# A two-layer hybrid decoder: where the recurrence's gate products stand, and which operand of the attention values is turned

## The chip, the core and the metric

The program runs on one core of a Trainium2 chip. The time is the device time of one execution in microseconds (us); lower is better. The kernel before took 3752.8 us, the median of three runs (3745.65 to 3756.24). One more execution was taken by the hardware profiler: 3757.68 us, of which the span from the first to the last instruction is 3756.1 us.

## The reference

Two groups of tokens, 256 of a prompt and 8 samples of 8 tokens (320 columns together), go through two layers of width 1024. Two places matter here. The first is the RWKV branch: 3328 columns of the input projection are mixed with the token before, and the last 256 of them feed three small products.

```python
mixed = (rwkv_cols + (prev - rwkv_cols) * p['rwkv_mu'][l]).astype(f32)
r, kc, vc, wd, ad, gd = jnp.split(mixed, RWKV_SPLITS, axis=-1)   # 1024, 1024, 1024, 64, 64, 128
w_log = -jax.nn.softplus(-(p['rwkv_w0'][l] + jnp.tanh(wd) @ p['rwkv_w_w2'][l])) - 0.5
decay = jnp.exp(-jnp.exp(w_log))
a_lr = jax.nn.sigmoid(p['rwkv_a0'][l] + ad @ p['rwkv_w_a2'][l])
g_rw = jax.nn.sigmoid(gd) @ p['rwkv_w_g2'][l]
```

The second is the cross attention, 4 heads of 256 dimensions over 256 memory tokens. The prompt has one memory, each of the 8 samples has its own:

```python
s = jnp.einsum('bthd,bmhd->bhtm', q, mk.astype(h.dtype)).astype(jnp.float32) * (X_HEAD_DIM ** -0.5)
pr = jax.nn.softmax(s, axis=-1).astype(h.dtype)
o = jnp.einsum('bhtm,bmhd->bthd', pr, mv.astype(h.dtype)).reshape(bsz, t, D_MODEL)
```

## The kernel before

Everything lies on chip with 128 features on the partitions and the 320 tokens along the row. A hardware loop runs over the two layers. The weights of a layer come as chunks of 128 output columns (512 KB) through a ring of four slots in the order of the table `SEGS`; SyncE issues the loads. For each chunk ScalarE makes `w_high` (L1330), then VectorE or GpSimd the remainder `w_low` (L1671, L662), and TensorE does 8 x 3 matmuls into one PSUM bank (L808 to L810, or L800, L801 and L805 for a chunk that takes its input in parts). Two split chunks are held (`AHEAD`), so a split starts when the matmuls of the chunk two before it are done (`chunk_done`).

In the segment `rwkv` (26 chunks) GpSimd makes `w_low`, and VectorE mixes the tokens straight from PSUM (`mix_tokens`, L1769 to L1774, five instructions; L1773 alone has both inputs in SBUF). Loops of four chunks drive all engines. The weights of the small products are two more chunks, `lora`, loaded into slots 2 and 3 of the ring. When all 26 chunks are mixed, ScalarE applies tanh and sigmoid to the last two (L1405, L1406), and TensorE computes the products for each of eight column tiles i (L911 to L913), with ScalarE's sigmoids (L1410, L1411) and VectorE's copy of the gate (L1779) behind each. Then VectorE, in `prepare_rwkv`, scales and scans the decay (L1798, L1800), computes `k * k_k` and its square (L1803, L1804), and so on to the recurrence. TensorE does 15 chunks of other projections beside it (`fill_rwkv`, L848 to L850): four, then the head sums of the square (L920), then six, further sums, then five. All fills use one PSUM bank, which ScalarE copies out (L1398). `prepare_rwkv` overwrites the place of the shift state, so it first waits until GpSimd's store of it (L693) has landed. GpSimd issues that store behind its `w_low` of the first two fills.

In the attention the work goes in units: 8 of the prompt (two token tiles by four heads) and 8 of the samples. Each has steps `s` (scores, L1236 or L1243), `max` and `p` on VectorE (L2151, L2152; L2155, L2156), `exp` and `t` on ScalarE (L1576, L1582), `t` on TensorE (transposes, L1251), and `o` (L1259 or L1266). The order on each engine is given by `att_steps`; on TensorE it is s(u+1), t(u), o(u). For a sample the four heads' scores lie in four strips of 32 partitions, 32 rows holding the queries of four samples, of which one's are wanted. The values of a sample are the stationary operand of `o`, in 8 tiles of 128 x 128, with 8 probability columns moving (L1266, N = 8). GpSimd loads keys and values of samples 0 to 3 ahead and issues those of sample 4 + j when `o` of sample j is done (L756, L757), 2 MB for each sample.

## Time and profile before

| | |
|---|---|
| median of three runs | 3752.8 us |
| profiled execution | 3757.68 us |
| its span | 3756.1 us |
| TensorE matmul busy | 3210.9 us (85%) |
| TensorE weight load busy | 2923.7 us (78%) |
| VectorE busy | 1952.9 us (52%) |
| ScalarE busy | 1165.8 us (31%) |
| GpSimd busy | 526.0 us (14%) |
| read from and written to HBM | 397.01 and 48.02 MB |

The profile reports busy time per engine, waits with the instruction that ended them, and the clock granted to TensorE (1.0 is 2.4 GHz, 0.5 is 1.2 GHz). A matmul of these 32-bit operands stands in the trace as two instructions where neither operand is split; order lists of the program count it once. Stages are told apart by line numbers.

### The profile page before, as it was taken

The page shows a single profiled execution, that of the slowest core. Times are in us where ns is not written, and L with a number is a line of the kernel's source. Part 1 is how long each engine was busy: PE and PEld are TensorE (multiplying, and loading weights), DVE is VectorE, ACT ScalarE, POOL GpSimd, SP SyncE. Part 2 cuts the span into 40 slices and gives each one's busy share as a digit, 9 for nine tenths or more (in the row PEclk, how much of TensorE's full clock was granted, in tenths as well). Part 3 has the DMA queues.
Part 4 walks back from the last instruction along what each step waited for, and adds up shares of the span by engine and source line. Part 5 has one row for each costly group of instructions (what it writes and reads, how often), then busy time and mean ns, then how long its engine had stood idle before and what let it go on. Part 6 is the DMA issues. An engine that isn't in the chain of part 4 may idle for free. (4 is left out here: it accounts for less than half of the span.)

```text
span 3756.1 us, 64350 instructions
## 1 busy us (share of the span) xinstructions
PE 3210.9 (85%) x25896; PEld 2923.7 (78%) x25896; DVE 1952.9 (52%) x2902; ACT 1165.8 (31%) x1579; POOL 526.0 (14%) x337
## 2 busy tenths in 40 slices
PE   8999788878877897899989888887788878978997
PEld 7989578577575897799989886775675768867997
DVE  4437565585565554144344476556753755541443
ACT  4432421141131443144344324111421214421442
POOL 0006310242210000000000164102422000000000
PEclk9999899887898999599989999999888979995999
DMA  4444210242262454234344443002422533532343
GB/s 159 150 135 139 92 38 3 68 141 85 61 254 109 143 189 148 90 124 150 118 140 149 134 135 100 24 24 70 150 74 81 212 151 124 187 128 112 130 149 104
DMA packets 119682, 448.03 MB, mean 119 GB/s; under 512 B 13648, under 2 KB 23920, under 8 KB 112176
## 3 DMA queue, kind: packets, MB, share of 16 engines
q1 hardware_dynamic: 98496, 331.84, 27.1%
q0 software_dynamic: 20976, 113.24, 7.7%
q8 instruction: 150, 2.46, 0.3%
q14 instruction: 60, 0.49, 0.1%
HBM read 397.01 MB, written 48.02 MB: 118 GB/s over the span
## 5 line engine op out<-in xcount | busy, mean ns | idle before, releaser
L808 PE MATMUL gemm_banks<-in_high,w_high 128*128 128x320 f32 (+1 forms) x2784 | 874.7, 314 | 76.8 <-POOL w_low L662 28.5
L1330 ACT ACTIVATE w_high<-ring 128x1024 fp32r<-128x1024 f32 x598 | 631.8, 1057 | 967.9 <-PE gemm_banks L810 633.2
L809 PE MATMUL gemm_banks<-in_low,w_high 128*128 128x320 f32 (+1 forms) x2784 | 863.0, 310 | 0.0
L810 PE MATMUL gemm_banks<-in_high,w_low 128*128 128x320 f32 (+1 forms) x2784 | 862.5, 310 | 0.0
L1671 DVE TENSOR_TENSOR w_low<-ring,w_high 128x1024 fp32r<-128x1024 f32 x436 | 533.9, 1225 | 543.8 <-ACT w_high L1330 539.9
L808 PEld LDWEIGHTS gemm_banks<-in_high,w_high 128*128 128x128 f32 x2784 | 531.9, 191 | 94.1 <-issue 74.1
L662 POOL TENSOR_TENSOR w_low<-ring,w_high 128x1024 fp32r<-128x1024 f32 x162 | 419.8, 2593 | 1139.3 <-ACT w_high L1330 623.9
L809 PEld LDWEIGHTS gemm_banks<-in_low,w_high 128*128 128x128 f32 x2784 | 532.3, 191 | 1.1
L810 PEld LDWEIGHTS gemm_banks<-in_high,w_low 128*128 128x128 f32 x2784 | 531.6, 191 | 0.0
L848 PE MATMUL gemm_banks<-in_high,w_high 128*128 128x320 f32 x640 | 227.5, 355 | 66.1 <-ACT stage L1398 41.5
L800 PE MATMUL gemm_banks<-in_high,w_high 128*128 128x320 f32 (+1 forms) x656 | 213.8, 338 | 68.6 <-ACT in_high L1346 65.3
L870 PE MATMUL gemm_banks<-act_high,w_high 128*128 128x320 f32 x704 | 224.7, 319 | 2.5 <-DVE arena L1723 2.5
L872 PE MATMUL gemm_banks<-act_high,w_low 128*128 128x320 f32 x704 | 217.6, 309 | 0.0
L871 PE MATMUL gemm_banks<-act_low,w_high 128*128 128x320 f32 x704 | 217.4, 309 | 0.0
L849 PE MATMUL gemm_banks<-in_low,w_high 128*128 128x320 f32 x640 | 212.7, 332 | 0.0
L850 PE MATMUL gemm_banks<-in_high,w_low 128*128 128x320 f32 x640 | 211.8, 331 | 0.0
L801 PE MATMUL gemm_banks<-in_high,w_low 128*128 128x320 f32 (+1 forms) x656 | 208.6, 330 | 0.0
L848 PEld LDWEIGHTS gemm_banks<-in_high,w_high 128*128 128x128 f32 x640 | 134.9, 211 | 90.6 <-issue 58.2
L800 PEld LDWEIGHTS gemm_banks<-in_high,w_high 128*128 128x128 f32 x656 | 135.9, 207 | 80.4 <-issue 74.3
L948 PE MATMUL gemm_banks<-arena 64*64 64x64 f32 x3264 | 139.1, 233 | 49.1 <-DVE arena L1861 38.0
L948 PEld LDWEIGHTS gemm_banks<-arena 64*64 64x64 f32 x3264 | 119.7, 146 | 62.7 <-DVE arena L1861 39.4
L1398 ACT ACTIVATE stage<-gemm_banks 128x320 f32<-128x320 f32 x80 | 35.0, 437 | 419.6 <-PE gemm_banks L850 319.4
(379 smaller groups left out, 4769.5 us busy)
## 6 DMA issues: line engine op xcount, KB each, us to landing
ring<-in_w SPq DMA_DIRECT2D x602, 512.0 KB, 3.4
arena<-in_kc POOLq DMA_DIRECT2D x16, 1024.0 KB, 5.0
arena<-in_vc POOLq DMA_DIRECT2D x16, 1024.0 KB, 7.2
out_fill<-stage SPq DMA_DIRECT2D x80, 160.0 KB, 3.8
arena<-out_fill POOLq DMA_DIRECT2D x4, 2560.0 KB, 12.0
arena<-in_ssm POOLq DMA_DIRECT2D x16, 512.0 KB, 10.5
out_s_ssm<-arena POOLq DMA_DIRECT2D x16, 512.0 KB, 7.0
arena<-in_ret POOLq DMA_DIRECT2D x16, 512.0 KB, 23.4
```

The source lines that it names most:

```text
L662: nc.gpsimd.tensor_tensor(w_low[:, slot], ring[:, pos % RING, 0:D], w_high[:, slot].bitcast(F32), ALU.subtract).then_inc(weights_split, 1)
L800: mm(dst, w_high[:, slot, w(k)], in_high[:, k, 0:n], start=(k == 0), stop=False)
L808: mm(dst, w_high[:, slot, w(k)], in_high[:, k, 0:n], start=(k == 0), stop=False)
L809: mm(dst, w_high[:, slot, w(k)], in_low[:, k, 0:n], start=False, stop=False)
L810: ins_ = mm(dst, w_low[:, slot, w(k)], in_high[:, k, 0:n], start=False, stop=(k == KT - 1))
L848: mm(dst, w_high[:, slot, w], in_high[:, k], start=(k == 0), stop=False)
L870: mm(dst, w_high[:, slot, w], act_high[:, k], start=(k == 0), stop=False)
L871: mm(dst, w_high[:, slot, w], act_low[:, k], start=False, stop=False)
L872: ins_ = mm(dst, w_low[:, slot, w], act_high[:, k], start=False, stop=(k == FT - 1))
L948: ins_ = mm(dst[r_], w[r_], src[r_], start=start, stop=stop)
L1330: f(w_high[:, slot], ring[:, s, 0:D], ACT.Copy).then_inc(weights_high, 1)
L1671: tt(w_low[:, slot], ring[:, pos % RING, 0:D], w_high[:, slot].bitcast(F32), ALU.subtract).then_inc(weights_split, 1)
```

## The change

It consists of two independent parts.

First, the chunks of `rwkv` are reordered so that the two with the inputs of the small products come first (`ORDER`), and the loops over them are written out. The weights of the small products get a buffer of their own (`lora_w`, over an unused part of the arena), loaded by one 1 MB DMA from GpSimd's queue ahead of the store of x; two empty places (`pad3`) take theirs in the ring. After chunks 4, 6, ... 18 TensorE does the product of tile i = 0 ... 7, always in banks 0 to 2, and waits for both readers of the product before. ScalarE's sigmoids and VectorE's gate copy stand after their work for the next chunk; the scale and the scan of tile i stand in VectorE's order one chunk later. `prepare_rwkv` begins with `k * k_k`.

Second, in `o` of a sample the probabilities are now the stationary operand (32 columns for each head) and the values move (N = 256). The output has tokens on the partitions, four heads in four strips, and the four samples of a group add into one PSUM bank, since VectorE multiplies the factor 1/sum by a 0/1 column (`own4`) that leaves only the sample's own rows. After four samples VectorE copies the bank (`ot`), TensorE turns it with two transposes (`turn`), and VectorE copies the result to its place. VectorE no longer waits for `o` in each unit.

```diff
 
-SEGS = [("ffa13", 2 * FT), ("ffa2", FT), ("pad2", 2), ("rwkv", RT), ("lora", 2), ("fill_rwkv", 20), ("ssm", 1 + CB), ("pad", 3),
+SEGS = [("ffa13", 2 * FT), ("ffa2", FT), ("pad2", 2), ("rwkv", RT), ("pad3", 2), ("fill_rwkv", 20), ("ssm", 1 + CB), ("pad", 3),
...
     first, step = {"P": ([("v", 0), ("v", 1), ("s", 0)], lambda u: [("s", u + 1), ("t", u), ("o", u)]),
-                   "V": ([("max", 0)], lambda u: [("p", u), ("max", u + 1), ("o", u)]),
+                   "V": ([("max", 0)], lambda u: [("p", u), ("max", u + 1)] + ([("o", u)] if u < 2 * NX else [])),
                    "A": ([("v", 0), ("v", 1), ("exp", 0)], lambda u: [("exp", u + 1), ("t", u)])}[engine]
-    return first + [s for u in range(n) for s in step(u) if s[1] < n]
+    out = list(first)
+    for u in range(n):
+        out += [s for s in step(u) if s[1] < n]
+        four = u >= 2 * NX and u % 4 == 3
+        if engine == "P" and (u == n - 1 or u == 2 * NX + 4):
+            out += [("turn", u - u % 4 - 1 if u < n - 1 else u)]
+        if engine == "V":
+            out += [("ot", u)] if four else []
+            out += [("o", 2 * NX + 3)] if u == 2 * NX + 5 else []
+            out += [("o", u)] if u == n - 1 else []
+    return out
...
         Btokbd = Kbd
+        lora_w = split(flat(arena[:, RT * T:RT * T + 2 * D].rearrange("p (a b) -> p a b", b=D)), 2, D)
...
                 pool.wait_ge(n_full.sem, n_full.value[("mix", PARTS[-1])])
+                pool.dma_start(lora_w, ins["lora"][l]).then_inc(dma["lora_here"][0], 16)
...
                     last_square_sum(seg)
+                    return
+                if seg == "rwkv":
+                    for c in range(count):
+                        chunk(c % RING, c, "last" if c == count - 1 else c == 0)
+                        if c in LORA_AT:
+                            lora(LORA_AT[c])
...
 
-            def lora():
-
-                b = BASE["lora"]
-                for s in (2, 3):
-                    pe.wait_ge(w_here[s], 16 * (b // RING + 1))
-                need(lora_act, "in")
-                pe.wait_ge(psum_free, RING + b)
-                for i in range(KT):
-                    if i >= 2:
-                        need(lora_act, i - 2)
-                        need(lora_g, i - 2)
-                    o, c = 3 * (i % 2), slice(i * P, (i + 1) * P)
-                    mm(bank(o)[:, 0:T], ring[0:64, 2, c], wdad[0:64, :], start=True, stop=True)
-                    mm(bank(o + 1)[:, 0:T], ring[64:128, 2, c], wdad[64:128, :], start=True, stop=True)
-                    hit(mm(bank(o + 2)[:, 0:T], ring[:, 3, c], gd, start=True, stop=True), lora_mm, i)
-                need(lora_act, KT - 1)
-                need(lora_g, KT - 1)
-                pe.sem_inc(chunk_done, 2)
+            def lora(i):
+
+                if i == 0:
+                    arrived(pe, layer, "lora_here")
+                    need(lora_act, "in")
+                else:
+                    need(lora_act, i - 1)
+                    need(lora_g, i - 1)
+                c = slice(i * P, (i + 1) * P)
+                mm(bank(0)[:, 0:T], lora_w[0:64, 0, c], wdad[0:64, :], start=True, stop=True)
+                mm(bank(1)[:, 0:T], lora_w[64:128, 0, c], wdad[64:128, :], start=True, stop=True)
+                hit(mm(bank(2)[:, 0:T], lora_w[:, 1, c], gd, start=True, stop=True), lora_mm, i)
...
                     kind, a, hd = UNITS[u]
+                    if name == "turn":
+                        need(V, ("ot", u))
+                        if a < 4:
+                            need(V, ("o", 2 * NX - 1))
+                        for d in range(2):
+                            ins_ = tr(bank(4 + a // 4)[:, d * P:(d + 1) * P], otok[:, a // 4, d * P:(d + 1) * P], K("ident"))
...
                         need(A, ("t", u))
-                        if u >= 2:
+                        if 2 <= u < 2 * NX:
...
                         else:
-                            for d in range(8):
-                                r0_ = 32 * (d // 2) + SL * (a % 4)
+                            for hd_ in range(NX):
+                                rows = slice(32 * hd_, 32 * hd_ + 32)
                                 for m in range(2):
-                                    ins_ = mm(bank(4 + u % 2)[:, d * SL:(d + 1) * SL], vc[a % 4][:, m, d * P:(d + 1) * P],
-                                              probT[:, u % 2, m, r0_:r0_ + SL], start=(m == 0), stop=(m == 1))
+                                    ins_ = mm(bank(6 + a // 4)[rows, 0:NMEM], probT[:, u % 2, m, rows],
+                                              vc[a % 4][:, m, hd_ * NMEM:(hd_ + 1) * NMEM],
+                                              start=(a % 4 == 0 and m == 0), stop=(a % 4 == 3 and m == 1),
+                                              tile_position=(0, 32 * hd_), skip_group_check=True)
...
 
-            def lora():
-                first_weights("fill_rwkv")
-                act_.wait_ge(psum_free, evacuated["rwkv"])
-                A_(f(wdad[0:64, :], wdad[0:64, :], ACT.Tanh))
-                A_.mark(f(gd, gd, ACT.Sigmoid), lora_act, "in")
-                for i in range(KT):
-                    need(lora_mm, i)
-                    o = 3 * (i % 2)
-                    A_(f(LW[:, i], bank(o)[:, 0:T], ACT.Sigmoid, bias=PR("w0", i)))
-                    A_.mark(f(Aa[:, i], bank(o + 1)[:, 0:T], ACT.Sigmoid, bias=PR("a0", i)), lora_act, i)
+            def rwkv_columns():
+                b = BASE["rwkv"]
+                for c in range(RT):
+                    weights(0, RING, SPLIT[RANK[b] + c + AHEAD])
+                    if c == 2:
+                        act_.wait_ge(psum_free, RING + b + 2)
+                        A_(f(wdad[0:64, :], wdad[0:64, :], ACT.Tanh))
+                        A_.mark(f(gd, gd, ACT.Sigmoid), lora_act, "in")
+                    if c - 1 in LORA_AT:
+                        i = LORA_AT[c - 1]
+                        need(lora_mm, i)
+                        A_(f(LW[:, i], bank(0)[:, 0:T], ACT.Sigmoid, bias=PR("w0", i)))
+                        A_.mark(f(Aa[:, i], bank(1)[:, 0:T], ACT.Sigmoid, bias=PR("a0", i)), lora_act, i)
...
 
-            def lora():
-                for i in range(KT):
-                    need(lora_mm, i)
-                    V_.mark(copy(rw_g[:, i], bank(3 * (i % 2) + 2)[:, 0:T]), lora_g, i)
-                dve.sem_inc(psum_free, 2)
+            def rwkv_columns():
+
+                b = BASE["rwkv"]
+                V_.restart()
+                for c in range(RT):
+                    dve.wait_ge(chunk_done, b + c + 1)
+                    mix_tokens((b + c) % RING, ORDER[c]).then_inc(psum_free, 3 if c == RT - 1 else 1)
+                    if c - 1 in LORA_AT:
+                        i = LORA_AT[c - 1]
+                        need(lora_mm, i)
+                        V_.mark(copy(rw_g[:, i], bank(2)[:, 0:T]), lora_g, i)
+                    if c - 2 in LORA_AT:
+                        i = LORA_AT[c - 2]
+                        need(lora_act, i)
+                        V_(ts(LW[:, i], LW[:, i], -math.exp(-0.5), None, ALU.mult))
+                        ins_ = nc.vector.tensor_tensor_scan(LW[:, i], K("reset64"), LW[:, i], 0.0, ALU.mult, ALU.add)
+                        V_(ins_) if i < KT - 1 else V_.mark(ins_, pre_v, "c")
+                dve.wait_ge(psum_free, RING + b + RT + 2)
...
                 arrived(dve, layer, "shift_stored")
-                need(lora_act, KT - 1)
-                V_(ts(LW, LW, -math.exp(-0.5), None, ALU.mult))
-                for i in range(KT):
-                    ins_ = nc.vector.tensor_tensor_scan(LW[:, i], K("reset64"), LW[:, i], 0.0, ALU.mult, ALU.add)
-                    V_(ins_) if i < KT - 1 else V_.mark(ins_, pre_v, "c")
...
                         V_(nc.vector.reciprocal(arec[:, u:u + 1], asum[:, u:u + 1]))
+                        if kind == "s":
+                            V_(tt(arec[:, u:u + 1], arec[:, u:u + 1], K("own4")[:, a % 4:a % 4 + 1], ALU.mult))
                         V_.mark(ts(prob[:, u % 2], prob[:, u % 2], arec[:, u:u + 1], None, ALU.mult), V, ("p", u))
-                    if name == "o":
+                    if name == "ot":
                         need(M, ("o", u))
-                        src = bank(4 + u % 2)
-                        if kind == "p":
-                            V_.mark(copy(ao[:, 2 * hd:2 * hd + 2, a * P:(a + 1) * P],
-                                         src[:, 0:2 * P].rearrange("p (a b) -> p a b", b=P)), V, ("o", u))
-                        else:
-                            V_.mark(copy(ao[:, :, TP + a * SL:TP + (a + 1) * SL],
-                                         src[:, 0:8 * SL].rearrange("p (a b) -> p a b", b=SL)), V, ("o", u))
+                        V_.mark(copy(otok[:, a // 4], bank(6 + a // 4)[:, 0:NMEM]), V, ("ot", u))
+                    if name == "o" and kind == "p":
+                        need(M, ("o", u))
+                        V_.mark(copy(ao[:, 2 * hd:2 * hd + 2, a * P:(a + 1) * P],
+                                     bank(4 + u % 2)[:, 0:2 * P].rearrange("p (a b) -> p a b", b=P)), V, ("o", u))
+                    if name == "o" and kind == "s":
+                        need(M, ("turn", u))
+                        t0_ = TP + 32 * (a // 4)
+                        for d in range(2):
+                            ins_ = copy(ao[:, d:8:2, t0_:t0_ + 32],
+                                        bank(4 + a // 4)[:, d * P:(d + 1) * P].rearrange("p (a b) -> p a b", b=32))
+                            V_(ins_) if d == 0 else V_.mark(ins_, V, ("o", u))
```

Hunks that only adapt a list, a semaphore or the host's arrays are left out. Line numbers of the lists below are those of each version.

VectorE, end of the `rwkv` chunks, before: the last two chunks' mixing, the gate copies, then scale, scans and `k * k_k`.

```order
L1769 TENSOR_SCALAR arena<-gemm_banks,omu 128x320
L1770 SCALAR_TENSOR_TENSOR arena<-gemm_banks,par,arena 128x255
L1772 SCALAR_TENSOR_TENSOR arena<-gemm_banks,par,arena 128x8x7
L1773 SCALAR_TENSOR_TENSOR arena<-arena,par 128x8
L1774 TENSOR_SCALAR arena<-gemm_banks 128x9
L1779 COPY arena<-mixer_banks 128x320
L1779 COPY arena<-gemm_banks 128x320
...
L1798 TENSOR_SCALAR arena<-arena 128x2560
L1800 SCALAR_TENSOR_TENSOR arena<-const,arena 128x320 x8
L1803 TENSOR_SCALAR arena<-arena,par 128x320 x8
```

VectorE, one pair of chunks in the middle of `rwkv`, after (an odd chunk, then an even one):

```order
L1789 TENSOR_SCALAR arena<-gemm_banks,omu 128x320
L1790 SCALAR_TENSOR_TENSOR arena<-gemm_banks,par,arena 128x255
L1792 SCALAR_TENSOR_TENSOR arena<-gemm_banks,par,arena 128x8x7
L1793 SCALAR_TENSOR_TENSOR arena<-arena,par 128x8
L1794 TENSOR_SCALAR arena<-gemm_banks 128x9
L1806 COPY arena<-mixer_banks 128x320
L1789 TENSOR_SCALAR arena<-gemm_banks,omu 128x320
L1790 SCALAR_TENSOR_TENSOR arena<-gemm_banks,par,arena 128x255
L1792 SCALAR_TENSOR_TENSOR arena<-gemm_banks,par,arena 128x8x7
L1793 SCALAR_TENSOR_TENSOR arena<-arena,par 128x8
L1794 TENSOR_SCALAR arena<-gemm_banks 128x9
L1810 TENSOR_SCALAR arena<-arena 128x320
```

The gate copy now stands behind an odd chunk's mixing, and the scale (with its scan, L1811) behind an even one's; the block of copies, the scale of 2560 columns and the eight scans after the last chunk are gone.

TensorE, three sample units of the attention before (scores of the next, transposes, values):

```order
L1243 MATMUL mixer_banks<-arena 32x256 x8
L1251 MATMUL mixer_banks<-const,arena 128x128 x2
L1266 MATMUL gemm_banks<-arena 128x8 x16
L1243 MATMUL mixer_banks<-arena 32x256 x8
L1251 MATMUL mixer_banks<-const,arena 128x128 x2
L1266 MATMUL gemm_banks<-arena 128x8 x16
```

TensorE, the same place after, about the fifth sample:

```order
L1264 MATMUL mixer_banks<-arena 32x256 x8
L1272 MATMUL mixer_banks<-const,arena 128x128 x2
L1287 MATMUL gemm_banks<-arena 32x256 x8
L1249 MATMUL gemm_banks<-const,arena 128x128 x2
L1264 MATMUL mixer_banks<-arena 32x256 x8
L1272 MATMUL mixer_banks<-const,arena 128x128 x2
```

Sixteen matmuls with 8 moving columns have become eight with 256 in strips of 32 partitions, the form of the scores; the two extra transposes come once in four samples.

## Rows read from the trace of the kernel before

**Rows 1.** The page: busy us by engine, share of the span, instructions.
```profile
PE 3210.9 (85%) x25896; PEld 2923.7 (78%) x25896; DVE 1952.9 (52%) x2902; ACT 1165.8 (31%) x1579; POOL 526.0 (14%) x337
```

**Rows 2.** Windows: start:end, length, busy by engine, granted clock, DMA share, GB/s.
```profile
1500.00:1513.00 13.00, 8.51 (x73) 5.87 (x72) 4.56 (x15) 2.84 (x9) 0.00 (x0) 0.97 0.00 1
1513.00:1540.00 27.00, 24.45 (x130) 20.91 (x134) 2.88 (x12) 1.89 (x6) 2.10 (x4) 0.50 0.40 156
1522.00:1524.00 2.00, 2.00 (x11) 2.00 (x11) 0.00 (x0) 0.00 (x0) 0.00 (x0) 0.50 1.02 430
```

**Rows 3.** TensorE in order of time, attention: start, length, line, tile, count.
```profile
1504.59 1.09 PE L1243 MATMUL mixer_banks<-arena 128*32 128x256 f32 x16
1507.58 1.16 PE L1259 MATMUL gemm_banks<-arena 128*128 128x128 f32 x8 [1.31 <-ACT arena L1582]
1508.67 1.09 PE L1243 MATMUL mixer_banks<-arena 128*32 128x256 f32 x16
...
1521.84 6.99 PE L1266 MATMUL gemm_banks<-arena 128*128 128x8 f32 x32 [1.27 <-ACT arena L1582]
1528.77 1.96 PE L1243 MATMUL mixer_banks<-arena 128*32 128x256 f32 x16
```

**Rows 4.** VectorE in order of time: the last copy of `o` in layer 1.
```profile
1592.02 0.22 DVE L2164 COPY arena<-gemm_banks 128x64 f32<-128x64 f32 x1 [8.37 <-PE gemm_banks L1266]
```

**Rows 5.** GpSimd in order of time: the first load of sample 4.
```profile
1518.71 0.53 POOL L756 DMA_DIRECT2D arena<-in_kc  x1 [45.41 <-PE gemm_banks L1266]
```

**Rows 6.** The page: DMA issues, KB each, median us to landing.
```profile
arena<-in_vc POOLq DMA_DIRECT2D x16, 1024.0 KB, 7.2
...
out_shift<-arena POOLq DMA_DIRECT2D x2, 117.0 KB, 2.2
```

**Rows 7.** TensorE in order of time: first matmul of an `rwkv` chunk that waited.
```profile
299.48 0.41 PE L808 MATMUL gemm_banks<-in_high,w_high 128*128 128x320 f32 x1 [0.19 <-POOL w_low L662]
```

**Rows 8.** ScalarE, then GpSimd, in order of time: splits of successive chunks.
```profile
295.80 1.06 ACT L1330 ACTIVATE w_high<-ring 128x1024 fp32r<-128x1024 f32 x1 [3.00 <-PE gemm_banks L805]
299.32 1.06 ACT L1330 ACTIVATE w_high<-ring 128x1024 fp32r<-128x1024 f32 x1 [2.46 <-PE gemm_banks L810]
303.30 1.06 ACT L1330 ACTIVATE w_high<-ring 128x1024 fp32r<-128x1024 f32 x1 [2.91 <-PE gemm_banks L810]
...
296.94 2.40 POOL L662 TENSOR_TENSOR w_low<-ring,w_high 128x1024 fp32r<-128x1024 f32 x1 [1.66 <-ACT w_high L1330]
```

**Rows 9.** VectorE and GpSimd in order of time, last `rwkv` chunk.
```profile
374.51 0.55 DVE L1769 TENSOR_SCALAR arena<-gemm_banks,omu 128x320 f32<-128x320 f32 x1 [1.54 <-PE gemm_banks L810]
375.92 1.97 DVE L1773 SCALAR_TENSOR_TENSOR arena<-arena,par 128x8 f32<-128x8 f32 x1
...
375.52 2.34 POOL L662 TENSOR_TENSOR w_low<-ring,w_high 128x1024 fp32r<-128x1024 f32 x1 [4.89 <-ACT w_high L1330]
...
381.54 0.57 POOL L693 DMA_DIRECT2D out_shift<-arena  x1
```

**Rows 10.** TensorE in order of time: two successive small products.
```profile
391.83 0.53 PE L911 MATMUL mixer_banks<-arena,ring 64*128 64x320 f32 x1
393.30 0.53 PE L911 MATMUL mixer_banks<-arena,ring 64*128 64x320 f32 x1
```

**Rows 11.** VectorE, then TensorE, in order of time: gate copy, `k * k_k`, head sums.
```profile
396.43 0.49 DVE L1779 COPY arena<-mixer_banks 128x320 f32<-128x320 f32 x1 [0.98 <-PE mixer_banks L913]
...
409.57 5.58 DVE L1803 TENSOR_SCALAR arena<-arena,par 128x320 f32<-128x320 f32 x8
...
420.15 5.34 PE L920 MATMUL mixer_banks<-arena,const 128*128 128x512 f32 x8 [2.42 <-DVE arena L1804]
```

**Rows 12.** ScalarE in order of time: copies of two successive fills.
```profile
404.60 0.44 ACT L1398 ACTIVATE stage<-gemm_banks 128x320 f32<-128x320 f32 x1 [4.32 <-PE gemm_banks L850]
408.98 0.44 ACT L1398 ACTIVATE stage<-gemm_banks 128x320 f32<-128x320 f32 x1 [2.99 <-PE gemm_banks L850]
```

**Rows 13.** GpSimd in order of time: what follows the store of x.
```profile
281.32 0.56 POOL L688 DMA_DIRECT2D arena<-in_conv  x1 [4.92 <-DMA out_x<-arena]
```

29 lines of the change are left out of this document (13 added, 16 removed).

## The prediction

> **What bounds the kernel now.** I read the page first: TensorE is busy 85% of the span and every other engine far less [rows 1], so the question for each edit is whether it changes what TensorE does or waits for. Since a busy TensorE is not one at its peak, I then read the windows for its granted clock. The attention stands out: up to the first sample the clock is 0.97, and from there 0.50, which is the level of 1.2 GHz, with TensorE busy 24.45 of 27 us and the other engines idle [rows 2]. TensorE in order of time shows what it is busy with: `o` of a sample takes 6.99 us for 32 instructions of 8 columns, while the scores of a sample, 16 instructions, take 1.96 us at that clock and 1.09 us at the full one [rows 3]. From 1521.84 + 6.99 to the next unit is a period of 10.8 us (the 7.0 of `o`, 1.96 of scores, 1.8 of transposes and waits). The stage ends with VectorE's copy at 1592.02 + 0.22 = 1592.24 [rows 4].
>
> The other place is `rwkv`. Its 26 chunks end at T0 = 374.51, the start of the last mixing [rows 9]. The head sums that open the second part of the preparation start at 420.15, and are released by VectorE's square (L1804), not by TensorE's four fills, 2.42 us idle before [rows 11]. So the 45.6 us after T0 are ruled by a chain of ScalarE and VectorE: tanh, eight products, scans, `k * k_k`, square. Inside the projection TensorE leads: ScalarE starts each split as a chunk ends, and a chunk that did not wait takes 299.32 - 295.80 = 3.52 us. Each second one takes 303.30 - 299.32 = 3.98 [rows 8], since it waits for GpSimd's split, with the restart behind it [rows 7]: 0.46 us in a pair of 7.50.
>
> **The attention.** The new `o` is 8 matmuls with 32 stationary columns and 256 moving ones, the very form of the scores. I price it at the 1.09 us of those [rows 3]. Bounds: at the lower clock 1.96; if strips of 32 did not run beside each other, four times 1.09 = 4.4. Not below 1.09, as nothing in the row is cheaper. A prompt unit with `o` of 1.16 us has a period of 1508.67 - 1504.59 = 4.08 us [rows 3]; ordering and waits of a sample unit are the same, so I take 4.1. VectorE's added multiply of one column lies in the 2 us while TensorE does `o` and the next scores; without that cover it is a short instruction, at most 0.2 us. The copy that VectorE waited for in each unit goes.
>
> Now the loads are late next. A sample's keys and values are 2 MB, at 430 GB/s [rows 2] 4.9 us. First landing: `o` releases GpSimd's issues, the first takes 0.53 us [rows 5], and the second load lands 7.2 us after its own issue [rows 6]; with 0.1 for the handover that is 7.8. The first new `o` starts where the old one did, 3 us behind the row of 1508.67, at 1511.7 (1507.58 - 1504.59 [rows 3]), and ends at 1512.8. The next three end 4.1 us apart: 1516.9, 1521.0, 1525.1. Sample 4 lands at 1520.6, in time; samples 5, 6 and 7 queue at 4.9 us: 1525.5, 1530.4, 1535.3. Scores of sample 5 so start 0.4 us late, at 1525.5; those of sample 6, with one `turn` (0.4) in between, at 1530.4, those of sample 7 at 1535.3 where TensorE was ready at 1534.5. Then one period (4.1) and a last transposes-to-`o` of 2.6 us: 1542.0. The tail is new: copy, two transposes, two copies, with their handovers, 1.9 us. End 1543.9 against 1592.24, that is 48.3; I take 48 us for a layer, 96 for both. If the clock stays at the lower level, a period is 1.96 + 1.96 + 1.9 = 5.8 us, longer than the loads', and the end is 1511.7 + 2.0 + 7 x 5.8 + 3.5 = 1557.8: 34.4 a layer.
>
> The page "DMA: Bandwidth & Descriptors" of the Trainium skill, section "Where 436 GB/s comes from", has the HBM side bind at about 358 GB/s for one core, which speaks against the change: an estimate by it is 5.9 us for a sample, and the sum would lose 3 us a layer. The trace differs, with 430 GB/s over 2 us, and I go by the trace.
>
> **The projection of `rwkv`.** Added on TensorE: eight products at 393.30 - 391.83 = 1.47 us [rows 10], 11.8 us. Before each but the first, TensorE waits for VectorE's gate copy. An odd chunk ends at t. GpSimd's split for the chunk after next starts at t + 1.14 and takes 2.40 [rows 8]. VectorE's mixing reaches L1773 at t + 1.41 (375.92 against 374.51), and that instruction then ends with the split: 375.92 + 1.97 = 377.89 against 375.52 + 2.34 = 377.86 [rows 9]. So mixing ends at t + 3.8, the copy of 0.49 us [rows 11] at t + 4.3, while TensorE is done with the even chunk at t + 3.52. The wait is 0.9 us, seven times: 6.3. Bounds: 0, if L1773 were not held, and 2.5 if GpSimd's split is held in turn by the scan and ends a scan later. I take 0.9. The 0.46 us wait for a split is covered in these eight pairs, since TensorE is 2.4 us longer: -3.7. Scales and scans of the tiles fit, as a pair now takes 7.04 + 1.47 + 0.9 = 9.4 us and VectorE needs 2 x 3.8 + 0.5 and about 1.1 of it for scale and scan. ScalarE's two sigmoids for a tile come behind the split of the next chunk, in the 2.4 us in which it is idle; tanh and two table loads delay one split by 1 us under TensorE's queue of two. If that cover is gone, each costs its own 1.1 us.
>
> On GpSimd's queue the new 1 MB load stands ahead of the store of x, and the conv load and the first split of the loop wait until that store has landed, at 281.32 [rows 13]. 1 MB at 430 GB/s is 2.4 us, the issue 0.56: I take 3.0 us later, between 0.6 (issue alone) and 6 (a transfer of its own in full before the store starts). TensorE holds two split chunks then and no more, so I count all of it. Two ring loads of 512 KB go, which were nobody's wait.
>
> The page "SBUF — State Buffer" of the Trainium skill, section "SBUF: two separate sides", calls what L1773 shows an exclusive lock, held for the whole instruction by whichever of VectorE and GpSimd is first. The trace agrees to 0.03 us. By that rule the new scales and scans can also hold up GpSimd.
>
> Sum: 11.8 + 6.3 - 3.7 + 3.0 = 17.4 us later at T0, for a layer. Bounds: 11.8 - 3.7 + 0.6 = 9, and 11.8 + 17.5 + 6 = 35.
>
> **The preparation.** VectorE's part before `k * k_k` goes: 409.57 [rows 11] would become T0 + 3.6. But the store of the shift state is late next. GpSimd issues it at 381.54, T0 + 7.0, behind the splits of two fills [rows 9]; it lands 2.2 us later [rows 6]. So VectorE starts at T0 + 9.3, needs 10.6 us as before (409.57 to 420.15), and has the square at T0 + 19.9. TensorE's four fills: the first split ends at 377.86, T0 + 3.35 [rows 9]; first fill done T0 + 6.9; then one fill in 408.98 - 404.60 = 4.38 us [rows 12]: T0 + 20.0. The two meet, and the head sums start at T0 + 20.2 instead of T0 + 45.6. All behind them hangs on them in the same order. 25.4 us gained, or between 20 (a store that lands 5 us later) and 30 (both quicker).
>
> Net for a layer: 25.4 - 17.4 = 8.0 us faster; for both 16. With the attention, 96 + 16 = 112 us. The profiled execution took 3757.68 us, 1.6 more than its span, and would take 3645.7; it lies 4.9 above the median of the runs, 3752.8, which gives 3640.8. Forecast: 3641 us.
>
> **Rivals.** First, the lower clock stays in the attention. For it: it had 0.50 through all sample units, and the scores were in them. Against: where prompt units and two samples' scores ran, with TensorE busy 8.5 of 13 us, it was 0.97 [rows 2]. Time: 3752.8 - 68.8 - 16 = 3668.
>
> The page "TensorE: Matmul & The Clock Gate" of the Trainium skill, section "HAM oscillation — how this bites in real kernels", tells of waits for loads that send the clock down in each round; the waits that I work out are under 1 us, so it weighs little.
>
> Second, the `rwkv` part gives nothing: VectorE and GpSimd hold each other up, T0 moves to the upper bound, and 35 - 25 = 10 us are lost a layer. For it the two-input instructions added beside the splits; against it VectorE's room of 9.4 us a pair. Time between 3657 (no gain) and 3752.8 - 96 + 20 = 3677.
>
> Third, loads of different samples do not overlap, and each takes the 7.8 us from release to landing. Sample 7 then lands at 1512.8 + 4 x 7.8 = 1544.0, 8.7 us later in each layer: 3658. Against it, the queue moved 430 GB/s within one.
>
> Fourth, slower. The seven waits of TensorE within `rwkv` and its late start let the clock fall to 1.2 GHz there, and it stays. A chunk of 24 matmuls then needs twice 3.52 us, 26 chunks 92 us more in a layer, against the 56 that the sum gains there: 3752.8 + 2 x 36 = 3825. It decides when over 16 of the 26 chunks run so. Against it: the waits are 0.9 us in 9.4, and TensorE was not kept at the lower clock by the waits of 0.46.
>
> **From the cases to the numbers.** Forecast 0.62, first rival 0.12, second 0.17, third 0.06, fourth 0.03. The forecast's own range is 3620 (attention 50, preparation 30 with T0 at its lower bound in part) to 3655. The range of 8 in 10 takes in the first two rivals: 3620 to 3680. A difference of 0.3% (11 us) is what a measurement tells from none. All but the fourth lie over 0.3% faster: faster 0.96, same 0.01, slower 0.03.
>
> **What would show it.** In the attention: `o` of a sample at 1.1 us and a clock above 0.9; samples 1 to 3 at 4.1 us, later ones near 4.9, with short waits for key and value loads; the stage 48 us shorter. In `rwkv`: TensorE waits of 0.9 us for the gate copy, pairs of 9.4 us between chunks 5 and 19, L1773's successor ending with GpSimd's split, conv load 3 us later after the store of x, and head sums 20 us after the last chunk, with `k * k_k` behind the landing of the shift store. It is wrong if sample units stay at 5.8 us or more, if T0 moves by over 25 us, or if the head sums start later than T0 + 25.

## The result and the profile after

The changed kernel takes 3663.6 us (median of four runs, 3662.5 to 3667.8), the kernel before 3753.5 in the same session: a ratio of 0.9766, 95% interval 0.9749 to 0.9783, or 90 us less. The forecast was 3641 us, 112 less, with a range of 3620 to 3680. The profiled execution took 3663.6 us, its span is 3662.0 where it was 3756.1. Other sessions had the kernel before at 3751.7 (the one with the first four experiments), 3745.9 (the next four) and 3746.4 us (the last three), so medians of different sessions can differ by 8 us; each ratio is taken within one session.

The page after, busy us by engine and share of the span, as in [rows 1]:

```profile
PE 3108.0 (85%) x25648; PEld 2827.5 (77%) x25648; DVE 1961.0 (54%) x2928; ACT 1164.8 (32%) x1579; POOL 525.6 (14%) x339
```

TensorE lost 103 us of busy time, and the shares hardly moved: the shares alone would not tell what the change did.

**The attention of the first layer after**, windows (columns as in [rows 2]), and then TensorE in order of time, as in [rows 3]:

```profile
1504.00:1512.00 8.00, 4.69 (x68) 2.62 (x68) 2.51 (x10) 2.20 (x7) 2.12 (x4) 1.00 0.51 177
1512.00:1520.00 8.00, 3.65 (x50) 1.75 (x50) 2.29 (x9) 1.55 (x6) 1.66 (x4) 0.99 0.98 385
1520.00:1522.00 2.00, 0.00 (x0) 0.00 (x0) 0.07 (x1) 0.00 (x0) 0.45 (x1) 0.50 0.98 414
1522.00:1530.00 8.00, 6.53 (x52) 2.65 (x52) 1.25 (x5) 0.95 (x3) 0.00 (x0) 0.50 0.90 379
1530.00:1540.00 10.00, 5.79 (x79) 2.86 (x72) 3.51 (x13) 2.28 (x7) 0.00 (x0) 1.00 0.02 7
```

```profile
1508.84 1.09 PE L1287 MATMUL gemm_banks<-arena 128*32 128x256 f32 x16 [1.51 <-ACT arena L1607]
1512.69 1.09 PE L1287 MATMUL gemm_banks<-arena 128*32 128x256 f32 x16 [1.51 <-ACT arena L1607]
1514.63 0.66 PE L1264 MATMUL mixer_banks<-arena 128*32 128x256 f32 x8 [0.85 <-DMA arena<-in_vc]
1517.60 1.10 PE L1287 MATMUL gemm_banks<-arena 128*32 128x256 f32 x16 [1.50 <-ACT arena L1607]
1522.22 1.96 PE L1264 MATMUL mixer_banks<-arena 128*32 128x256 f32 x16 [3.52 <-issue]
1526.05 1.96 PE L1287 MATMUL gemm_banks<-arena 128*32 128x256 f32 x16 [1.25 <-ACT arena L1607]
```

(The view ended within the scores of 1514.63 and so shows 8 of their 16 instructions.)

`o` takes 1.09 us, a unit 3.85 (1512.69 - 1508.84), and the clock is full in these units. Then the scores of sample 5 wait 3.5 us with TensorE at rest. The page names no releaser there ("issue"); the DMA share of 0.98 in those two us says what was late, and the issue rows (KB, us to landing) settle it:

```profile
arena<-in_kc POOLq DMA_DIRECT2D x1, 1024.0 KB, 5.3
arena<-in_vc POOLq DMA_DIRECT2D x1, 1024.0 KB, 6.9
...
arena<-in_vc POOLq DMA_DIRECT2D x1, 1024.0 KB, 11.0
...
arena<-in_vc POOLq DMA_DIRECT2D x1, 1024.0 KB, 12.0
```

With their issue times, the values of samples 4 to 7 land at 1514.5, 1522.2, 1527.0 and 1531.9. Behind the wait TensorE runs at 0.50, 1.2 GHz, for one unit and a half.

**The start of the projection after**: GpSimd's queue [rows 13], then TensorE's third chunk.

```profile
276.22 0.56 POOL L700 DMA_DIRECT2D arena<-in_lora  x1 [2.83 <-DVE arena L1712]
276.78 0.56 POOL L701 DMA_DIRECT2D out_x<-arena  x1
287.47 0.54 POOL L703 DMA_DIRECT2D arena<-in_conv  x1 [10.14 <-DMA out_x<-arena]
```

```profile
290.44 0.64 PE L823 MATMUL gemm_banks<-in_high,w_high 128*128 128x320 f32 x1 [7.29 <-POOL w_low L676]
```

The store of x landed in 10.0 us and not in 4.7. The conv load was issued 6.15 us later than before, and the third chunk, begun after 7.3 idle us, ran in part at the lower clock. From the waits (total us, times, longest) and the timeline of the preparation (TensorE, VectorE):

```profile
PE mixer_banks L929 <- DVE arena L1806: 12.6, 14, 0.9
```

```profile
400.96 0.60 PE L869 MATMUL gemm_banks<-in_high,w_high 128*128 128x320 f32 x1 [3.69 <-DVE arena L1794]
...
421.18 3.59 PE L935 MATMUL mixer_banks<-arena,const 128*128 128x512 f32 x8
```

```profile
406.99 5.43 DVE L1831 TENSOR_SCALAR arena<-arena,par 128x320 f32<-128x320 f32 x8 [6.18 <-DMA out_shift<-arena]
412.46 2.83 DVE L1832 TENSOR_TENSOR arena<-arena 128x2560 f32<-128x2560 f32 x1
425.75 2.29 DVE L1835 TENSOR_SCALAR arena<-mixer_banks 128x2048 f32<-128x2048 f32 x1 [10.47 <-PE gemm_banks L935]
```

The seven waits of 0.9 us in a layer are there as forecast. T0 is 397.3 now. VectorE begins `k * k_k` at T0 + 9.7, released by the shift store (forecast 9.3), and has the square at T0 + 18.0 (forecast 19.9). But the head sums start at T0 + 23.9 and not at T0 + 20.2, behind the fourth fill [rows 11: the square ended last before]. The first fill began at T0 + 3.7, close to the forecast, but after 3.7 idle us and at the lower clock, and was done at T0 + 10.2 (forecast 6.9).

The stretches, in us, from VectorE's rows of each trace (first mixing, T0, first instruction behind the head sums, memset at the start of the recurrence; first maximum to the end of the last copy of the attention), layer 1 / layer 2:

| | before | attention alone | rwkv alone | changed |
|---|---|---|---|---|
| first mixing to T0 | 94.7 / 94.7 | 94.7 / 94.7 | 117.7 / 117.5 | 117.6 / 118.1 |
| T0 to head sums done | 51.9 / 51.2 | 48.8 / 51.3 | 28.4 / 26.2 | 28.4 / 26.6 |
| on to the recurrence | 65.4 / 61.0 | 65.5 / 60.9 | 61.7 / 65.5 | 61.7 / 65.8 |
| attention | 118.0 / 118.7 | 73.3 / 73.3 | | 76.1 / 76.0 |

From before to changed these stages give 85.3 us of the 94.1 between the two spans. Most of the rest (6 us) lies between the recurrence and the attention, where neither part of the change is: both layers together take 1959.5 us there in the profile of before and 1953.5 in the changed kernel's, but 1946.3 in that of `wide_o` (below), whose code there is that of before. So a single profiled execution carries several us that no edit explains.

### The profile page after: what moved, and what is told of

It reads as the page before. It is cut to its first block and busy times, and to the rows that moved or that the text cites. A ratio compares the mean times of both kernels' runs of the same rounds, so it can differ in the third digit from the quotient of the medians.

```text
span 3662.0 us, 63366 instructions
## 1 busy us (share of the span) xinstructions
PE 3108.0 (85%) x25648; PEld 2827.5 (77%) x25648; DVE 1961.0 (54%) x2928; ACT 1164.8 (32%) x1579; POOL 525.6 (14%) x339
## 5 line engine op out<-in xcount | busy, mean ns | idle before, releaser
L824 PE MATMUL gemm_banks<-in_low,w_high 128*128 128x320 f32 (+1 forms) x2864 | 890.0, 311 | 0.0
L824 PEld LDWEIGHTS gemm_banks<-in_low,w_high 128*128 128x128 f32 x2864 | 549.5, 192 | 2.4
L825 PEld LDWEIGHTS gemm_banks<-in_high,w_low 128*128 128x128 f32 x2864 | 548.7, 192 | 0.0
L815 PE MATMUL gemm_banks<-in_high,w_high 128*128 128x320 f32 (+1 forms) x576 | 185.9, 335 | 65.8 <-ACT in_high L1368 65.6
## 6 DMA issues: line engine op xcount, KB each, us to landing
arena<-out_fill POOLq DMA_DIRECT2D x4, 2560.0 KB, 11.8
```

The lines of the kernel that those rows point to most:

```text
L815: mm(dst, w_high[:, slot, w(k)], in_high[:, k, 0:n], start=(k == 0), stop=False)
L824: mm(dst, w_high[:, slot, w(k)], in_low[:, k, 0:n], start=False, stop=False)
L825: ins_ = mm(dst, w_low[:, slot, w(k)], in_high[:, k, 0:n], start=False, stop=(k == KT - 1))
```

## The experiments

**One part at a time.** `att_alone` is the kernel before with the second part of the change only, `rwkv_alone` with the first only. In short:

```diff
 # att_alone
-  vc[a % 4][:, m, d * P:(d + 1) * P], probT[:, u % 2, m, r0_:r0_ + SL]
+  probT[:, u % 2, m, rows], vc[a % 4][:, m, hd_ * NMEM:(hd_ + 1) * NMEM]
 # rwkv_alone
+  if c in LORA_AT:
+      lora(LORA_AT[c])
```

> The kernel before with the attention of the change alone; the recurrence part stays as it was. Theory A (read from the two traces): the attention gives 41.9 us in the first layer and 43.4 in the second, because the load of sample 5's values lands at 1522.2, 7.7 us after sample 4's and not 4.9, and the unit behind that wait runs at 1.2 GHz. Then 85 us less than before: 3668 us. Rival B (the working of the prediction, with the missing gain lost elsewhere): 96 us less, 3657. If the two parts help each other, this run gives less than 85 us.

> The kernel before with the recurrence part of the change alone (products, decay, scans between the chunks, own weight buffer); the attention stays as it was. Theory A: the projection ends 23 us later in a layer (7.9 at its start, 15 through the products), the preparation gives 23.5 to 24.5 back at the head sums, so the part is worth only what follows from layer to layer: 0 to 9 us in all, 3744 to 3753 us. Rival B (the prediction): 16 us, 3737. Rival C: the part costs time, over 3757.

Measured: `att_alone` 3662.5 us, ratio 0.9764 (0.9748 to 0.9780); `rwkv_alone` 3752.0, ratio 0.9997 (0.9985 to 1.0008). The attention is the whole gain, and the first part is worth nothing: its theory A holds, and my 16 us for it are outside the interval. For the attention, 89 us (82 to 95 by the interval) agree with theory A's 85 and not with 96; its stages are 90 us shorter in the table. Its stage is 3 us shorter here (73.3) than in the changed kernel (76.1) with the same code. In the first layer, the first `o` of a sample starts 38.2 us into the stage here and 40.1 in the changed kernel, and 35.1 and 36.0 us follow it. TensorE's granted clock from 1496 to 1502, in the prompt units, is 1.00 here and 0.50 there:

```profile
1496.00:1502.00 6.00, 4.76 (x34) 2.89 (x30) 1.86 (x7) 0.95 (x3) 0.00 (x0) 0.50 0.01 3
```

The loads also meet other units. Here the scores of sample 4 wait for them, 1.88 us and not 0.85, and those of sample 5 do not:

```profile
1515.17 1.94 PE L1260 MATMUL mixer_banks<-arena 128*32 128x256 f32 x16 [1.88 <-DMA arena<-in_vc]
```

**The weights' load behind the conv load.**

```diff
-                pool.dma_start(lora_w, ins["lora"][l]).then_inc(dma["lora_here"][0], 16)
                 pool.dma_start(outs["x"], x).then_inc(dma["x_stored"][0], 16)
                 arrived(pool, l, "x_stored")
                 pool.dma_start(conv_s, ins["conv"][l]).then_inc(dma["conv_here"][0], 16)
+                pool.dma_start(lora_w, ins["lora"][l]).then_inc(dma["lora_here"][0], 16)
```

> The changed kernel with the 1 MB load of the products' weights issued by GpSimd behind the conv load, so behind the landing of the store of x, and not ahead of it. Theory A: the store of x lands in 4.7 us again and not in 10.0; the conv load is issued near 281.3, TensorE's 7.3 us wait before the third chunk falls to about 1, and that chunk runs at full clock: 7.9 us in a layer, 16 in both: 3648 us. Rival B: the ring loads of 1 MB that start at 279.9 share the engines with the store and with this load, and the split or the first product waits in its place: under 6 us, over 3657. Rival C: the products' weights land too late for chunk 4, and the wait moves there: no gain, 3663.

Measured: 3655.7 us, 0.9742 (0.9728 to 0.9757). GpSimd's queue:

```profile
276.21 0.56 POOL L700 DMA_DIRECT2D out_x<-arena  x1 [2.47 <-DVE arena L1712]
281.70 0.56 POOL L702 DMA_DIRECT2D arena<-in_conv  x1 [4.93 <-DMA out_x<-arena]
282.29 0.53 POOL L703 DMA_DIRECT2D arena<-in_lora  x1
```

The store lands in 4.8 us, TensorE's wait is 1.8 us, and T0 comes 7.2 and 6.3 us earlier after the first mixing (110.4 / 111.8). The mechanism of theory A is shown by the trace. Of those 13.5 us the span kept 6.3 and the ratio 9 (its interval overlaps the changed kernel's), so the time came out near rival B's bound, but not for B's reason. Part of the rest is a step of VectorE in the first layer's preparation (2.1 us, below). The attention is 3 us shorter, and the stages that the edit does not touch are 8 us longer: 4.3 ahead of the first mixing, 3.5 between the recurrence and the attention. No run says why; it is of the size by which `wide_o` and before differ with the same code.

**The gate copy ahead of the mixing.**

```diff
-                    dve.wait_ge(chunk_done, b + c + 1)
-                    mix_tokens((b + c) % RING, ORDER[c]).then_inc(psum_free, 3 if c == RT - 1 else 1)
                     if c - 1 in LORA_AT:
                         i = LORA_AT[c - 1]
                         need(lora_mm, i)
                         V_.mark(copy(rw_g[:, i], bank(2)[:, 0:T]), lora_g, i)
+                    dve.wait_ge(chunk_done, b + c + 1)
+                    mix_tokens((b + c) % RING, ORDER[c]).then_inc(psum_free, 3 if c == RT - 1 else 1)
```

> The changed kernel with VectorE's gate copy of a tile ahead of the mixing of the next chunk and not behind it. Theory A: TensorE's 14 waits of 0.9 us for that copy go, a pair of chunks with a product takes 8.55 us and not 9.48, and the projection ends 6.3 us earlier in each layer: 12.6 us, 3651. Rival B: the wait of TensorE for GpSimd's split, 0.46 us in a pair, which the products covered, comes back: 6 us, 3657. Rival C: ScalarE's sigmoids become what the product waits for: under 3 us, 3661 or more.

Measured: 3650.8 us, 0.9740 (0.9728 to 0.9753), 12.8 us less by the spans and 10 by the ratios, whose intervals just touch: theory A. A pair with a product takes 8.51 us, the 14 waits are gone, and T0 comes 6.0 and 6.7 us earlier.

**Keys and values loaded apart.**

```diff
-                for b in SAMPLES[4:]:
-                    pool.wait_ge(at["P"].sem, at["P"].value[("o", 8 + b - 4)])
-                    load_kv(b)
+                for b, name in ((4, "s"), (5, "s"), (4, "o"), (6, "s"), (5, "o"), (7, "s"), (6, "o"), (7, "o")):
+                    pool.wait_ge(at["P"].sem, at["P"].value[(name, 8 + b - 4)])
+                    (load_k if name == "s" else load_v)(b)
```

> The changed kernel with keys and values of samples 4 to 7 on semaphores of their own: the keys are loaded as soon as the scores that read the old ones are done, the values as before after `o`, and TensorE waits for the keys before the scores and for the values before `o`. Theory A: the attention's missing 5 us a layer are the load of sample 5 (a wait of 3.5 us, one of 0.9, and a unit and a half at 1.2 GHz behind them). With the first load some 6 us earlier these go, each unit takes 3.85 us, and the stage is 7.6 us shorter: 15 us in both layers, 3648. Rival B: the loads are bound by bytes and by their order, `o` now waits for values where scores waited for keys: under 6 us, over 3657. Rival C: the clock falls for another reason than that wait, the unit of sample 5 stays at 1.2 GHz though nothing waits: 9 us, 3655.

Measured: 3654.4 us, 0.9757 (0.9744 to 0.9771), which overlaps the changed kernel's interval: by the ratios the gain is 3 us and not clear of noise, so the times don't decide between the theories. The trace shows the mechanism. TensorE and windows:

```profile
1511.97 1.09 PE L1294 MATMUL gemm_banks<-arena 128*32 128x256 f32 x16 [1.58 <-ACT arena L1614]
...
1515.89 1.10 PE L1294 MATMUL gemm_banks<-arena 128*32 128x256 f32 x16 [1.58 <-ACT arena L1614]
1516.75 1.11 PE L1270 MATMUL mixer_banks<-arena 128*32 128x256 f32 x16
1520.19 1.09 PE L1294 MATMUL gemm_banks<-arena 128*32 128x256 f32 x16 [1.36 <-ACT arena L1614]
```

```profile
1504.00:1512.00 8.00, 4.71 (x70) 2.98 (x72) 2.63 (x12) 1.90 (x6) 2.12 (x4) 1.00 0.93 349
1512.00:1520.00 8.00, 4.72 (x68) 2.87 (x68) 2.75 (x11) 1.85 (x6) 1.06 (x2) 1.00 1.01 423
1520.00:1530.00 10.00, 6.38 (x87) 3.72 (x88) 3.53 (x14) 1.95 (x7) 0.00 (x0) 1.00 0.30 120
```

No wait for a load is left, the clock is 1.00 in all these units, and the stage takes 69.9 and 71.1 us instead of 76.1 and 76.0: 11 us by the trace, 12 by the span, of theory A's 15. Rival C falls for sample 5, whose lower clock went with the wait. But a load wait is not the only thing that comes before a lower clock: here too TensorE is at 0.50 from 1496 to 1500, in the prompt units, and at 0.59 and 0.50 in the last unit of the second layer (3341 to 3347), with no idle time over 1.8 us ahead of either. Those stretches are left open.

**No empty ring places; three fills.** In `no_pads` the four empty places around the chunks are gone, and the first fill waits for chunk 23's bank only:

```diff
-SEGS = [("ffa13", 2 * FT), ("ffa2", FT), ("pad2", 2), ("rwkv", RT), ("pad3", 2), ("fill_rwkv", 20), ("ssm", 1 + CB), ("pad", 3),
+SEGS = [("ffa13", 2 * FT), ("ffa2", FT), ("rwkv", RT), ("fill_rwkv", 20), ("ssm", 1 + CB), ("pad", 3),
...
-                    pe.wait_ge(psum_free, RING + pos)
+                    pe.wait_ge(psum_free, RING + pos - (2 if seg == "fill_rwkv" and c == 0 else 0))
```

> The changed kernel without the two pairs of empty ring places around the chunks of rwkv, so that the weights of the first fill are loaded two chunks earlier; its first fill also waits for the mixing of chunk 23 instead of the last one. Theory A: the first fill starts with the end of the last chunk instead of 3.7 us behind it and at full clock, the shift store is issued at T0 + 3.5 instead of T0 + 7.3, and the head sums, which now wait for the fourth fill at T0 + 22 to 24, start at T0 + 17: 5 to 7 us in a layer, 12 in both, 3651. Rival B: what is gained ahead of the head sums is given back behind them, where VectorE's instructions with two inputs and GpSimd's splits hold each other up: under 6 us, over 3657.

```diff
 # fills_3, on TensorE (ScalarE's order follows)
-                fill("fill_rwkv", 4)
+                fill("fill_rwkv", 3)
                 need(pre_v, "kksq")
                 tile_sums(pre_p, "kkss", K("bones"), E3)
-                fill("fill_rwkv", 6)
+                fill("fill_rwkv", 7)
```

> The changed kernel with three fills and not four ahead of the head sums on TensorE, and seven behind them and not six. Theory A: the head sums wait for the fourth fill and no longer for VectorE's square; with three they start at T0 + 19 to 20 in both layers, as the prediction had it: 4.4 us and 1.9 us, together 6, 3657. Rival B: the square is the later one, no gain, 3663. Rival C: the fill moved behind delays the exponential that releases VectorE: slower than 3664.

Measured: `no_pads` 3655.4 us, 0.9744 (0.9722 to 0.9766); `fills_3` 3656.7, 0.9765 (0.9748 to 0.9782). Neither interval is clear of the changed kernel's, and by the ratio `fills_3` gives nothing (6.9 us by the span). In the traces the head sums are done 21.6 and 26.6 us behind T0 with `no_pads`, 23.1 and 26.1 with `fills_3`, against 28.4 and 26.6. So the fourth fill was the late one in the first layer (theory A's 4.4 us came out as 5.3), but in the second VectorE's square is nearly as late (0.5 us, and not 1.9). Up to the recurrence `no_pads` then loses what it gained: from the first mixing 207.2 and 212.4 us, against 207.7 and 210.5. Its rival B's mechanism holds; the time, 3655.4, lies between A's 3651 and B's 3657.

**What stretches VectorE.** `no_lock` lets GpSimd split 8 of 1024 columns of all fills of the preparation but the first two, and leaves out the low half of the other 1016.

```diff
-                fill("fill_rwkv", AHEAD, PREP_FILLS + AHEAD)
+                fill("fill_rwkv", AHEAD, PREP_FILLS + AHEAD, 8)
```

> The changed kernel in which GpSimd's split of the fills of the preparation (all but the first two) covers 8 of its 1024 columns, so the low half of those weights is left out; everything else stays. Theory A: VectorE's long instructions of the preparation are stretched in steps of 2.1 us (2.83 to 4.93, 5.4 to 7.4, 8.6 to 10.7) by nothing but the splits that GpSimd runs at that time, between one and four of them in a layer, by chance of phase. Then all of them take their short time in both layers (the square and the decay product 2.83, the eight products with r_k under 8.7), both preparations have the same length, and the end comes 2 to 5 steps earlier: 4 to 10 us, 3654 to 3660. Rival B: the stretch is the DMA traffic or something else in VectorE: the steps stay, and the time too.

Measured: 3648.5 us, 0.9730 (0.9706 to 0.9753). VectorE and the split beside it in the changed kernel's second layer, and then VectorE in `no_lock`'s:

```profile
2262.87 5.04 DVE L1841 SCALAR_TENSOR_TENSOR arena<-arena 128x2560 f32<-128x2560 f32 x1
2267.95 10.69 DVE L1843 SCALAR_TENSOR_TENSOR arena<-arena,par 128x320 f32<-128x320 f32 x8
...
2262.82 2.41 POOL L676 TENSOR_TENSOR w_low<-ring,w_high 128x1024 fp32r<-128x1024 f32 x1 [3.13 <-ACT w_high L1352]
```

```profile
2254.86 2.83 DVE L1841 SCALAR_TENSOR_TENSOR arena<-arena 128x2560 f32<-128x2560 f32 x1
2257.72 4.67 DVE L1843 SCALAR_TENSOR_TENSOR arena<-arena,par 128x320 f32<-128x320 f32 x8
```

Every stretched instruction is short now, and T0 to the recurrence takes 78.3 and 78.2 us, the same in both layers, where it was 90.1 and 92.4. Theory A is shown for the cause of the stretches and was too low for the size: 26 us over both layers, with VectorE busy 37 us less there. Not all 26 need be the stretches, since the edit also makes the splits short for TensorE, whose fills had waited 6.4 and 2.0 us for them in the changed kernel. The span kept 13.4; between the recurrence and the attention, where the edit changes next to nothing, this execution was 11 us longer.

**Was it the columns?** `wide_o` is the kernel before with 32 moving columns in `o` instead of 8.

```diff
-                                r0_ = 32 * (d // 2) + SL * (a % 4)
+                                r0_ = 32 * (d // 2)
-                                    ins_ = mm(bank(4 + u % 2)[:, d * SL:(d + 1) * SL], vc[a % 4][:, m, d * P:(d + 1) * P],
-                                              probT[:, u % 2, m, r0_:r0_ + SL], start=(m == 0), stop=(m == 1))
+                                    ins_ = mm(bank(4 + u % 2)[:, d * 32:(d + 1) * 32], vc[a % 4][:, m, d * P:(d + 1) * P],
+                                              probT[:, u % 2, m, r0_:r0_ + 32], start=(m == 0), stop=(m == 1))
```

> The kernel before with 32 instead of 8 moving columns in each matmul of `o` of a sample (the rows of all the sample's tokens of a head, of which 8 are kept): four times the columns through the same 16 stationary tiles. Theory A: what kept the clock at 1.2 GHz in the attention is that TensorE streamed so few columns; with four times as many it rises, `o` takes 3.5 us in place of 7.0, and the two stages give about 60 us: 3692. Theory B: a matmul of `o` costs its stationary tile, 0.22 us for 8 columns or for 32, and the clock stays at 0.50: 3752, as before.

Measured in one execution: 3740.7 us, against 3741.0 to 3758.2 of the kernel before in the same session.

```profile
1528.07 7.04 PE L1266 MATMUL gemm_banks<-arena 128*128 128x32 f32 x32 [1.28 <-ACT arena L1582]
```

7.04 us for 32 columns, 6.99 for 8 [rows 3], a clock of 0.50, and attention stages of 117.1 and 119.0 us (118.0 and 118.7 before): theory B. At that clock `o` cost its 32 instructions with their stationary tiles. The change has half as many, with 32 stationary columns. At the same clock that takes `o` from 6.99 to 1.96 us; the full clock takes another 0.87 us off it and 0.87 off the scores. Why the clock is full beside the new `o` and 0.50 beside the old one, no run here says: more moving columns in the old form did not bring it back.

**Together.** `combo` has the five edits; `combo2` goes back to four fills and puts GpSimd's first split of the loop ahead of its wait for the store of x.

```diff
 # combo2 against combo
                 pool.dma_start(outs["x"], x).then_inc(dma["x_stored"][0], 16)
+                weights(0, RING, BASE["rwkv"] + AHEAD)
...
-                stream("rwkv", RT)
+                splits(pool, weights, BASE["rwkv"] + 1, RT - 1, lambda i, c: None)
```

> The changed kernel with five edits together: the load of the products' weights behind the conv load, the gate copy ahead of the mixing, keys and values loaded apart, no empty ring places, three fills ahead of the head sums. Theory A: what the single edits gave or should give adds up (8, 13, 15 and, the last two together, 12 us): 48 us under the changed kernel, 3615. Rival B: the three edits in the recurrence part share one bound (VectorE and GpSimd holding each other up in the preparation), and only about half of their 33 us is kept: 3632.

> The combination (3617 us) with four fills again ahead of the head sums, and with GpSimd's first split of the loop ahead of its wait for the store of x. Theory A: with three fills TensorE stood idle 7.55 us ahead of the head sums and did them at 1.2 GHz (5.3 us and not 3.6); the fourth fits into that gap and leaves one less behind, 2 to 4 us a layer; the third chunk starts 7.3 us behind the first and not 9.2, 2 us a layer. Together 8 to 12 us, 3607. Rival B: VectorE rules the preparation anyway, and only the 4 us of the start are kept: 3613.

Measured: `combo` 3617.3 us, 0.9660 (0.9646 to 0.9673); `combo2` 3614.2, 0.9634 (0.9614 to 0.9654). Both beat the changed kernel clearly; between the two the intervals overlap. By its median `combo` is at theory A (3615), by its ratio at 40 us of the 48, between A and B; its span, 3610.2, is 52 under the changed kernel's, and those of the five single edits add up to 46. By the ratios it is 40 against 31, and with the noise of both the time does not exclude rival B. The trace does: from the first mixing to the recurrence both layers together are 24.5 us shorter, and 6.3 more are gained ahead of the first mixing, where the empty places were, 31 us where B had about half of 33. The edits share a little in the first stretch (30 us singly, 24.5 together). For `combo2` rival B holds: the first mixing to T0 is 1.5 us shorter (102.0 against 103.6 and 103.5), but the head sums start at T0 + 20.2 in both, with four fills or three, since VectorE's square is the later one (rows of `combo`):

```profile
390.41 7.40 DVE L1839 TENSOR_SCALAR arena<-arena,par 128x320 f32<-128x320 f32 x8 [6.03 <-DMA out_shift<-arena]
```

```profile
400.73 5.30 PE L940 MATMUL mixer_banks<-arena,const 128*128 128x512 f32 x8 [7.55 <-DVE arena L1840]
```

`k * k_k` is stretched to 7.40 us, and TensorE waits 7.55. In the second layer the head sums are done 2.6 us earlier with four fills (T0 + 24.9 and not 27.5), since they ran at the full clock there: 3.70 us and not 6.38.

## Why the prediction was right, and where its size was off

The direction and most of the size came out, and none of the signs of being wrong did. But 3663.6 us lies outside the forecast's own range (3620 to 3655) and inside that of the second rival (3657 to 3677, chance 0.17); it is within 3620 to 3680 only because that range took the rivals in. One of the two parts worked as forecast, the other was worth nothing.

- **The attention, mechanism right, 48 us became 42 and 43.** `o` at 1.09 us, the full clock and the stage's new form came as forecast; a unit took 3.85 and not 4.1 us. The term that was mis-sized is "samples 5, 6 and 7 queue at 4.9 us". I had taken the 430 GB/s of a 2 us window for the whole queue, and let the landings follow each other at that rate. The four loads moved 8.4 MB from 1508 to 1529, 400 GB/s on the mean and 356 to 385 between 1512 and 1518, and sample 5 landed 7.7 us behind sample 4. The rate explains little of it: at 400 GB/s 2 MB take 5.2 us. Estimated from the windows, the bytes of samples 4 and 5 were through at 1513.8 and 1519.3, and the two landed 0.7 and 2.9 us behind that. At the end of the queue one sees such a tail: after 1529 the rate falls from 115 GB/s to 33 at 1531, and sample 7 lands at 1531.9. What holds back the last of the 16 engines is open. The late landing made a wait of 3.5 us where I had 0.4. I had given the clock little weight because my waits were under 1 us; the clock fell in this one. `kv_split` takes both away. Of the 6.4 us missing in the first layer 3.8 lie behind the first `o` of a sample, and 2.6 ahead of it, in prompt units that ran partly at 0.50 (1496 to 1502); the prediction had no term for those. The Trainium skill, page "DMA: Bandwidth & Descriptors", section "Where 436 GB/s comes from", gives about 358 GB/s as the limit from HBM, by my estimate 3 us a layer. The mean measured lies between that and my figure, so the rate cost less than the page's figure would have; what was lost came by the late landing and the clock.
- **The projection, 17.4 became 23.** Products (11.8) and waits (6.3 minus 3.7) came as worked out: `early_copy` took exactly the waits away. The failed term is "I take 3.0 us later" for the store of x. The conv load came 6.15 us later, past my upper bound of 6, and the third chunk's mixing 7.8 and 8.3 us, because two ring loads of 512 KB (issued at 279.9 and 283.4) shared the engines too, 3.1 MB in all in the store's 10 us, and because the chunk behind the idle time ran at the lower clock. `late_lora` gives 7.2 and 6.3 us of it back.
- **The preparation, 25.4 became 23.5 and 24.6 against the profile of before, at the end of the head sums.** The step "first fill done T0 + 6.9" failed (T0 + 10.2): I had its split in time, but not the restart of TensorE at the lower clock after 3.7 idle us. "All behind them hangs on them in the same order" failed too. Behind the head sums the stretch to the recurrence takes 61 or 65 us in all four columns of the table, by which of VectorE's instructions meet a split.
- **The sum**: 8 us a layer for the first part became 0, shown by `rwkv_alone`. That was my second rival in its mild form ("no gain", 3657), with the price partly from another place: the start and the first fill more than VectorE and GpSimd. The other 6 us above 3657 are the attention's. The first rival (the lower clock in all sample units) and the fourth (slower) did not come. The third, loads that don't overlap, came in part: 7.7 us between samples 4 and 5, 4.8 and 4.9 between the others.
- **The yardstick.** In the first layer of the profile of before, T0 to the head sums took 51.9 us; in `att_alone`, with the same code there, 48.8, since VectorE's square took 2.82 us and not 4.92. So a sum against one profiled execution carries 2 or 3 us a layer there that no edit explains. The measured 90 us is nearer to the forecast's 112 than the 85.3 us of the stages that were worked out; that difference is luck and no merit of the working.

## What to carry to other kernels

Ask of each transfer that is moved which other transfers are in flight until it lands, and add up all their bytes, not the one that stands ahead of it. A late load can cost more than its wait: behind 3.5 us (and in `att_alone` behind 1.9) the next unit ran at the lower clock, with 1.96 us for `o` and not 1.09. The 14 waits of 0.9 us for the gate copy cost their own time, which is what `early_copy` gave back. When work is taken off a chain, look at once for what stands in the other engine's order ahead of the next meeting point: here four fills and a small store stood there, and the gain of one part was used up by them and by a later start.
